# A transformer block on one core: 1/rms taken off the rows of x and put on behind the first projections

## The reference

```
h = x
h = h + hybrid_mixer(rms_norm(h, norm_mix), w_in, conv, w_rg, w_ig, lru_lambda, ..., w_out)
h = h + memory_cross_attention(rms_norm(h, norm_cross), mem, norm_mem, w_xq, w_xkv, w_xo)
h = h + hier_moe(rms_norm(h, norm_ffn), routers, w_gate_up, w_down)       # 32 experts, top 2
return rms_norm(h, norm_final)

def rms_norm(x, g):  x * rsqrt(mean(x * x) + 1e-6) * g

hybrid_mixer:  x_lru, g_lru, q, k, v = split(xn @ w_in)      # 5 blocks of 512 columns
    y_lru = rg_lru(causal_conv(x_lru)) * gelu(g_lru);  y_att = attention(rope(q), rope(k), v)
    return concat(rms_norm(y_lru), rms_norm(y_att)) @ w_out
```

## Time and profile before

| | |
|---|---|
| median of three runs | 664.78 us (664.26 to 666.75) |
| the profiled execution's own time | 664.22 us |
| its span, first to last instruction | 662.4 us |
| busy: PE, DVE, ACT, POOL | 504.6, 234.2, 181.6, 20.7 us |
| moved by DMA | 238.08 MB, 359 GB/s on average |
| share of the chain that ended last | PE 47%, DMA 45%, DVE 3%, ACT 2% |

### The profile page before, as it was taken

The page is one execution under the profiler, slowest core; times in us unless marked ns, Lnnn a source line. Parts: engine busy times, 40 slices in busy tenths (PEclk is TensorE's granted clock), DMA queues, the critical chain, the costliest instruction groups (busy, mean ns, idle before and its releaser), DMA issues.

```text
span 662.4 us, 13318 instructions
## 1 busy us (share of the span) xinstructions
PE 504.6 (76%) x5802; PEld 369.0 (56%) x5802; DVE 234.2 (35%) x518; ACT 181.6 (27%) x399; POOL 20.7 (3%) x21
## 2 busy tenths in 40 slices
PE   3999999999999887886656856666686666558654
PEld 3988998789888665654323523343353334335422
DVE  3796897664644632221111211121121112112203
ACT  6559567364442112120100011110001111000203
POOL 2000111200000000000000000000000000000000
PEclk9999999999999999999888977897897789889989
DMA  8655834396579799999999999999999999999993
GB/s 352 285 191 190 319 138 164 137 395 243 186 283 355 287 380 426 427 435 435 431 425 431 440 436 436 427 430 430 430 427 436 448 436 427 430 412 427 427 422 134
DMA packets 15716, 238.08 MB, mean 359 GB/s; under 512 B 1728, under 2 KB 1856, under 8 KB 3008
## 3 DMA queue, kind: packets, MB, share of 16 engines
q1 hardware_dynamic: 15536, 237.03, 86.0%
q10 hardware_dynamic: 144, 0.52, 0.2%
HBM read 236.49 MB, written 1.05 MB: 359 GB/s over the span
## 4 chain that ended last, share of the span: by engine, by line
PE 47%; DMA 45%; DVE 3%; ACT 2%; issue 1%; another core or an unknown queue 1%; POOL 1%; SPq 0%; ACTq 0%; DVEq 0%
DMA ring<-in_w_expert 44%; PE psum L610 15%; PE psum L596 11%; PE psum L885 9%; PE psum L916 4%; PE psum L857 1%; DMA landing<-in_dense 1%; PE psum L767 1%; PE psum L744 1%; PE psum L579 1%; PE psum L844 1%; PE psum L909 1%; DVE small L1769 1%; DVE small L1771 1%
## 5 line engine op out<-in xcount | busy, mean ns | idle before, releaser
L885 PE MATMUL psum<-ring,xg 128*32 128x256 f32 x2048 | 152.4, 459 | 90.9 <-DMA ring<-in_w_expert 84.6
L885 PEld LDWEIGHTS psum<-ring,xg 128*32 128x32 f32 x2048 | 73.6, 130 | 158.0 <-DMA ring<-in_w_expert 90.6
L610 PE MATMUL psum<-split_w,split_act 128*128 128x512 f32 x432 | 101.9, 393 | 1.2 <-DVE res L1544 1.2
L610 PEld LDWEIGHTS psum<-split_w,split_act 128*128 128x128 f32 x432 | 80.3, 188 | 18.4 <-DVE res L1544 1.6
L1230 ACT ACTIVATE small<-psum 128x128 f32<-128x128 f32 x32 | 8.9, 278 | 284.1 <-PE psum L885 284.1
L1769 DVE SCALAR_TENSOR_TENSOR small<-small,psum 128x128 f32<-128x128 f32 x32 | 9.2, 288 | 203.8 <-ACT small L1230 203.8
L1356 DVE TENSOR_TENSOR split_w<-landing,split_w 128x2048 fp32r<-128x2048 f32 x29 | 66.2, 2289 | 30.9 <-ACT split_w L1031 30.9
L596 PE MATMUL psum<-split_act,split_w 128*128 128x256 f32 x576 | 70.1, 284 | 1.1 <-DVE split_act L1369 1.1
L1031 ACT ACTIVATE split_w<-landing 128x2048 fp32r<-128x2048 f32 x30 | 57.3, 1914 | 49.3 <-PE psum L610 26.0
L596 PEld LDWEIGHTS psum<-split_act,split_w 128*128 128x128 f32 x576 | 69.5, 192 | 1.8 <-DVE split_w L1390 1.3
L1780 DVE COPY ybuf<-psum 32x128 f32<-32x128 f32 x128 | 37.3, 291 | 74.5 <-PE psum L916 73.6
(11 more groups left out here) (182 smaller groups left out, 342.8 us busy)
## 6 DMA issues: line engine op xcount, KB each, us to landing
ring<-in_w_expert SPq DMA_DIRECT2D x20, 6144.0 KB, 48.2
ring<-in_w_expert SPq DMA_DIRECT2D x23, 2048.0 KB, 34.3
landing<-in_dense SPq DMA_DIRECT2D x30, 1024.0 KB, 5.5
ring<-in_w_expert SPq DMA_DIRECT2D x26, 1024.0 KB, 8.2
res<-in_x SPq DMA_DIRECT2D x2, 512.0 KB, 3.6
work<-in_mem SPq DMA_DIRECT2D x1, 1024.0 KB, 11.7
ybuf<-in_late SPq DMA_DIRECT2D x1, 512.0 KB, 14.4
after_routing<-in_norm_final SPq DMA_DIRECT2D x1, 512.0 KB, 13.2
```

The source lines that it names most:

```text
L610: i = mm(b, src[t][:, k0 + k, P * h:P * h + P], w[a][:, k, :], start=first and k == 0 and n == 0, stop=last and k == CT - 1 and n == 2)
L885: i = mm(half[SLOTS * strip:SLOTS * strip + SLOTS], xg[:, CT * part + k, SLOTS * j:SLOTS * j + SLOTS], w[:, k, :, P * strip:P * strip + P] ...
```

## The change

- x is turned as it lands, unscaled: PE starts its 16 transposes straight from `res`, the first eight when the first 128 tokens are there. `scale_half(1, ...)` and the tile `xtok` are gone.
- 1/rms is put on where results leave PSUM: for q, k and v as ACT's scale for each token, which costs no instruction. For the channel results the tokens lie along the free dimension, so a row of 256 values is made first. DVE writes two diagonal tiles (`rstd_diag`), PE multiplies them with ones (job `rows`, bank 0), ACT copies the result (`rstd_rows`), and DVE multiplies xl0, xl1, gl0 and gl1 by it as it reads them (`times_rstd`). Before, ACT copied xl0, gl0 and gl1, and DVE xl1.
- Dense half 0 is loaded, split and used in two pieces of 512 KB. Both low parts are DVE's; POOL has none.
- `ident` and the parameters (200 columns) are loaded by a DMA that ACT issues, the other 580 columns of `ctab` later by SP.
- ACT sums the squares of the second half of x behind `split_hi(1)`, those of the first half before `turned_hi`.
- PE turns the memory behind q, not ahead of it, and DVE scales it behind `split_lo(3)`.

Core of the diff:

```
@@ sync
+            sp.dma_start(landing[:, 0:HALF // 2], dense[0][:, 0:HALF // 2]).then_inc(raw_first, 16)
+            sp.dma_start(landing[:, HALF // 2:HALF], dense[0][:, HALF // 2:]).then_inc(raw_loaded[0], 16)
             load_half(1)
+            sp.dma_start(ctab[:, 0:FIRST], early[:, 0:FIRST]).then_inc(early_loaded, 16)
...
-            sp.wait_ge(w_lo_first, 1)
@@ tensor
+            pe.wait_ge(first_loaded, 16)
+            for h in range(NH):
+                pe.wait_ge(x_loaded[h], 16)
+                for c in range(4):
+                    for k in range(2):
+                        i = tr(pb(f"Tx{c}")[:, 256 * k + P * h:256 * k + P * h + P],
+                               res[:, h, (2 * c + k) * P:(2 * c + k + 1) * P], ident)
...
+            pe.wait_ge(w_lo_first, 1)
+            for m, k0 in ((0, 0), (0, CT), (1, 0)):
...
             pe.wait_ge(early_loaded, 16)
+            pe.wait_ge(diag_ready, 1)
+            end(mm(begin("rows")[:, 0:S], ones, rstd_diag, start=True, stop=True), "rows")
+            tokens_whole(2, ["q0", "q1"], xs_)
...
             turn("Tm", memraw)
-            tokens_whole(2, ["q0", "q1"], xs_)
@@ scalar
+            nc.scalar.dma_start(ctab[:, FIRST:], early[:, FIRST:]).then_inc(first_loaded, 16)
+            act.wait_ge(x_loaded[0], 16)
+            sum_squares(res, 1, (0,))
+            act.wait_ge(first_loaded, 16)
+            turned_hi("Tx", xs_, "norm_mix", (0,))
+            hi = slot(0, KC)[0]
+            act.wait_ge(raw_first, 16)
+            copy(hi[:, 0:CT], raw(0, KC)[:, 0:CT]).then_inc(w_hi_first, 1)
+            turned_hi("Tx", xs_, "norm_mix", (1,))
+            act.wait_ge(raw_loaded[0], 16)
+            copy(hi[:, CT:], raw(0, KC)[:, CT:]).then_inc(w_hi, 1)
+            turned_hi("Tx", xs_, "norm_mix", (2, 3))
...
-            plain("gl0", gx[:, 0:2])
...
-            plain("gl1", gx[:, 2:4])
@@ vector
+            turned_lo("Tx", xs_, "norm_mix", (0, 1))
...
+            V.tensor_tensor(lo[:, 0:CT], raw(0, KC)[:, 0:CT], hi[:, 0:CT].bitcast(F32), ALU.subtract).then_inc(w_lo_first, 1)
...
+                release(V.tensor_tensor(dst, pb(job).rearrange("p (c t) -> p c t", c=2),
+                                        rstd_rows.unsqueeze(1).to_broadcast([P, 2, S]), ALU.mult), job)
...
             split_lo(11)
+            times_rstd("gl0", gx[:, 0:2])
+            times_rstd("gl1", gx[:, 2:4])
             for t in range(CT):
                 i = V.tensor_tensor_scan(xc[:, t], decay[:, t], root[:, t], 0.0, ALU.mult, ALU.add)
```

## The result

The changed kernel takes 670.88 us (median of 4 runs, 670.35 to 671.62); beside it the kernel before took 665.46 (4 runs, 664.26 to 666.75). The ratio is 1.0081, with a 95% interval of 1.0063 to 1.0100. It is slower, by more than this measurement is uncertain, where no change was forecast, and 670.88 lies outside the range. The profiled execution took 670.35 us with a span of 668.6, 6.2 us more than the span before.

The account below looks back on a forecast made before the run. PE paces the front and DMA bytes bound the second half, so PE's time before the experts carries through. 2.7 - 1.7 - 0.45 - 0.1 = 0.45 us gained: 663.8 or 664.3, forecast 664.2 us, range 662.2 to 666.4.

Parts of the forecast that it names:

- I take 0.1.: Attention: the scan starts 2.1 us late behind DVE's reads of gl0 and gl1; PE loses 0.1 us, 1.5 if nothing absorbs it.
- the low part of the recurrence's output: Attention, DVE: the last instruction queued behind the scan that PE waits for; PE was to wait less than 0.5 us.
- The start: Front up to xl1, rows and the memory's transposes: PE done at 25.2 + 1.75 instead of 25.79 + 1.75, 0.55 us gained.
- Transposes near 4.4: Start of the kernel: x lands at 4.3 and 5.6 us, and PE's first transpose starts at 4.4, at 212 ns each.
- First products at 11.2: Start: first weight piece in at 6.9 us, so PE starts xl0 at 11.2 and not 13.92, 2.7 us gained.
- The clock's price: xl0 and xl1: after a rest of 3.4 us PE runs the first products at the low clock, costing 1.34 to 2.26, taken 1.7.
- The product with the row: Behind xl1: job rows, one 128x256 float32 product on PE, costs 0.45 us and ends at 25.2.
- Rival 1: Start and attention: slow stretch dearer or x late, DVE and attention at 0.5 each; sum -1.4, 666.0 us; chance 0.19.
- Rival 2: First products: the clock does not fall over the rest, xl1 ends 1.7 earlier, gain 2.1, 662.6 us; chance 0.17.
- Rival 3: Start: ACT's DMA with ident is served behind SP's, landing at about 10.6; slower by 5.7 us, 670; chance 0.06.
- rival 4: Whole kernel: more is won than the chain shows, over 3.3 us; chance 0.04.
- Carried through one for one: Before the experts: a microsecond won or lost by PE comes through to the end one for one, and nothing else does.

Follow-up runs that it names:

- the subtraction: The second kernel with half 12's low part, a DVE subtraction of two SBUF operands, moved up beside POOL's products; 670.52 us in one execution.
- the idle transposes: The second kernel with 22 idle transposes of ident on PE in the rest before the first products; 663.81 us, and 663.82 us when run again.
- the second kernel: The changed kernel with gl1 read behind the scans and not ahead of them; 665.44 us, ratio 0.9997 to the kernel before.
- the two kernels without the overlap: The changed kernel with POOL's gelu products waiting for DVE's scans, 665.21 us, and the changed kernel with gl1 read behind the scans, 665.44 us.

## Why the prediction was wrong

**The step that failed is the attention's: "I take 0.1."** I had counted what the new order does to DVE's own queue, 2.1 us of lateness, and bounded it at 1.5. That part held: with POOL kept away the kernel takes 665.21 us. But I took the scan's duration, 2.43 us, from a trace in which nobody worked beside it. The reads of gl0 and gl1 do not only delay the scan. They also release POOL, whose three instructions then begin 0.26 us after the first scan. In the trace of before, the same products stood at 79.71, 1.7 us behind the scans. I chose no row of POOL there and did not ask who else waits for what I was moving, though the program says it: POOL starts them when gl0 and gl1 have been read. The overlap adds 4.6 us to the scans, their queue carries it to half 12's low part, PE waits 2.75 us for that, and its next 96 products, at a granted clock of 0.87, take 1.5 longer. That is 4.25 of the 4.6 us that the two traces differ by between the scores and 200 us. The prediction had watched another instruction, the low part of the recurrence's output; for that one PE did not wait (it ended at 110.90, and PE asked at 110.96).

The Trainium skill, "SBUF — State Buffer" (section "Who interferes with whom"), says that a DVE instruction with two inputs in SBUF contends with a GpSimd instruction that reads SBUF, and that with one SBUF input DVE (outside its two-port modes) does not. The traces agree, with 7.05 against 2.43 us for the scans, 3.10 against 2.29 for the subtraction, and 1.28 and 1.21 unchanged for instructions with one such input. It was a rule that spoke against this change, and I did not weigh it.

**The start.** Its direction was wrong by a small sum, +0.55 forecast, about -0.9 measured against the profiled execution of before. Term by term:
- Transposes near 4.4: 4.70. x came 0.5 us later than before in this pair (ACT's first square at 4.50, had 4.00), where I had 0.3. Over all the profiled executions the medians are 4.40 and 4.08, so the term was about right.
- First products at 11.2: 12.21. The piece landed at 8.31 and not 6.9, so that ACT began on it at 8.34 and not at 7.45. I had divided bytes by a rate; the whole half lands at 8.22 or 8.95, so half the bytes did not land in half the time. Why not stays open.
- The clock's price, 1.34 to 2.26, taken 1.7: 2.2, at the upper end, by 14.07 against 11.87; 2.3 by the idle transposes. The products ran at the low level first, as forecast, and the size was 0.5 short. In the second kernel's profile the granted clock was 0.80 in the rest itself. In the changed kernel the sixteen transposes took 3.67 us, 0.23 each, which is about the low level throughout, so the clock may not have been up before the rest at all; idle work in it would then have raised it rather than held it.
- The product with the row took 0.45 in the sum, and PE was done with it 0.45 us after xl1 (26.28 to 26.73), and half 5's low part (42.11 to 44.39) held nobody up. Both held.

**Why 0.9 us late at the scores still gave an equal time** in the two kernels without the overlap: the profiled execution of before was a favourable one. Its start took 11.87 us where another execution of the same start took 13.73. Against its median, the changed front may lose less or nothing. That fits the rows, but only two executions of that start were profiled, so I call it likely, not shown.

**The rivals.** Rival 1 had a right cause at the start, the dearer stretch; its price, which is -1.3 when its terms are added up and not -1.4, holds the 0.9 that came. Rival 2, that the products start at full level, is refuted by 14.07. Rival 3 named 670 us and was wrong all the same: ACT's transfer had landed when PE began at 4.70, well before 10.6. That its number is nearly the measured one is luck; place and mechanism were others. Of rival 4, a gain of over 3.3 us, nothing came.

**Carried through one for one:** the lag of PE before the experts (about 6.15 us at 302.76) is the difference of the spans, 6.2, as the first paragraph of the prediction had it. But the way from the last dense products to the experts is not of one length: from the start of the last long row of products by rows to the first wait for an expert's DMA it took 101.35 us in the trace of before, 102.0 in that of the changed kernel, and 103.6 and 105.7 in two others. A gain of 1 us at the start is therefore smaller than what two executions differ by behind it, and only medians can show it.

## What to carry to other kernels

When an instruction is moved, look at everything that its semaphores release, on every engine, and lay the released work beside what will run then; a duration read from a trace holds only for the neighbours that it had there. An instruction that has grown though no wait is shown can be held by another engine: look for one that ends just before it does. If an engine has to rest ahead of a dense stretch, idle work in that rest can be worth more than the earlier start that made the rest, but measure it: here it paid in one start and not in the other, and in the one where it paid it wants repeated executions to be seen.

## What the runs showed that I had not expected

- Four scans of 128x256 take 2.43 us alone and 6.97 to 7.06 beside POOL's instructions, while POOL loses only 0.2 to 0.3 us on each of three. Where a subtraction of 128x2048 meets POOL instead, POOL loses more (1.05 to 2.97 us) and DVE 0.8. By the starts and ends, an instruction in both cases stands still until the other engine's is over, and its record shows that as duration, not as a wait.
- The first half of dense half 0, as a transfer of its own, landed at 8.09 to 8.51 us in six executions, the undivided 1 MB at 8.22 and 8.95 in two.
- With ACT's 100 KB transfer beside x, ACT's first square started at 4.37 to 4.57 us in nine executions; without it, at 4.00, 4.08 and 4.25. That is 0.3 us at the medians, close to the transfer's share of the bytes (0.26). What SP issues behind x differs too, and no run separates the two.
- The same start takes 11.87 us in one execution and 13.73 in another for the same 96 products. In the new start it is 14.04 to 14.08 in three executions and 13.26 in a fourth.
- The granted clock read 1.00 in a stretch where products took 0.22 us that take 0.12 otherwise; in another execution of the same start it read 0.81 over the 14.10 us.
